# Three feed-forward stages start their first gate block on x before the norm's division, with VectorE forming every low part

## What is computed

```
x = first_block(x)                    # ffn, mixer, ffn, final norm
for i in range(2):                    # second block
    mod = silu(c) @ mod_w[i] + mod_b[i]               # 1024 x 9216, one row
    sh1, sc1, g1, sh2, sc2, g2, sh3, sc3, g3 = split(mod, 9)
    h = rmsnorm(x, g) * (1 + sc) + sh
    x = x + 0.5 * g1 * ((silu(h @ Wg) * (h @ Wu)) @ Wd)   # 1024 -> 2816 -> 1024
    ...                               # mixer, second ffn of the layer
return rmsnorm(x, final_gain)
```

## Time and profile before

| | us |
|---|---|
| median of 3 runs | 1616.53 |
| the runs | 1615.57, 1616.53, 1620.67 |
| span of the profiled execution | 1619.2 |
| its own time | not listed apart; of the three runs only 1620.67 is above its span, 1.5 over it |
| PE busy in it | 1605.0 |
| DVE busy | 1221.3 |
| ACT busy | 807.2 |

### The profile page before, as it was taken

How to read it: one execution, slowest core, us unless ns; L and a number is a source line. 1 busy time by engine, 2 the same in 40 slices (tenths; PEclk the granted TensorE clock), 3 DMA queues, 4 the chain that set the end, 5 groups by cost and what they waited for, 6 DMA issues and landing times.

```text
span 1619.2 us, 33790 instructions
## 1 busy us (share of the span) xinstructions
PE 1605.0 (99%) x14157; PEld 1583.5 (98%) x14157; DVE 1221.3 (75%) x1382; ACT 807.2 (50%) x892; POOL 48.4 (3%) x81
## 2 busy tenths in 40 slices
PE   9999999999999999999999999999999999999998
PEld 9999999999999999999998999999999998899998
DVE  6888786676778878887777888877889578774544
ACT  5434567654644354443567654445444466654343
POOL 0000000000000000000000000000000010000000
PEclk9999999999999999999999999999999999999999
DMA  8788544444568865888453368874798535345551
GB/s 327 289 305 306 219 175 171 150 156 160 184 255 294 311 224 209 316 326 295 153 183 130 131 246 327 304 292 160 288 342 316 195 139 197 135 157 206 183 197 63
DMA packets 51066, 365.04 MB, mean 225 GB/s; under 512 B 5792, under 2 KB 5920, under 8 KB 7072
## 3 DMA queue, kind: packets, MB, share of 16 engines
q1 hardware_dynamic: 40176, 287.03, 48.5%
q0 software_dynamic: 10368, 75.50, 12.8%
q10 hardware_dynamic: 432, 1.20, 0.2%
HBM read 362.65 MB, written 1.05 MB: 225 GB/s over the span
## 4 chain that ended last, share of the span: by engine, by line
PE 95%; DVE 2%; ACT 1%; DMA 1%; issue 1%; DVEq 0%; SPq 0%; ACTq 0%
PE bank L261 54%; PE bank L297 27%; PE bank L253 3%; PE bank L280 2%; PE bank L2149 1%; PE bank L384 1%; DVE wlo L192 1%; PE bank L395 1%; DMA raw<-stream_in 0%; PE bank L1652 0%; PE bank L429 0%; PE bank L2195 0%; PE bank L2101 0%; PE bank L2119 0%; PE bank L1130 0%
## 5 line engine op out<-in xcount | busy, mean ns | idle before, releaser
L261 PE MATMUL bank<-xh,whi 128*128 128x256 f32 x2608 | 725.3, 278 | 1.3 <-DVE wlo L192 1.3
L261 PE MATMUL bank<-xl,whi 128*128 128x256 f32 x2608 | 721.6, 277 | 0.0
L261 PE MATMUL bank<-xh,wlo 128*128 128x256 f32 x2608 | 721.5, 277 | 0.0
L192 DVE TENSOR_TENSOR wlo<-raw,whi 128x2048 fp32r<-128x2048 f32 x254 | 580.9, 2288 | 180.5 <-ACT whi L184 180.2
L184 ACT ACTIVATE whi<-raw 128x2048 fp32r<-128x2048 f32 x253 | 482.8, 1913 | 277.3 <-PE bank L261 166.4
L261 PEld LDWEIGHTS bank<-xh,whi 128*128 128x128 f32 x2608 | 489.9, 188 | 2.6 <-DVE wlo L192 1.7
L261 PEld LDWEIGHTS bank<-xl,whi 128*128 128x128 f32 x2608 | 490.3, 188 | 0.1
L261 PEld LDWEIGHTS bank<-xh,wlo 128*128 128x128 f32 x2608 | 489.9, 188 | 0.0
L297 PE MATMUL bank<-hid_hi,whi 128*128 128x256 f32 x1056 | 292.1, 277 | 0.0
L297 PE MATMUL bank<-hid_lo,whi 128*128 128x256 f32 x1056 | 291.6, 276 | 0.0
L297 PE MATMUL bank<-hid_hi,wlo 128*128 128x256 f32 x1056 | 291.6, 276 | 0.0
(11 more groups left out here) (392 smaller groups left out, 1842.8 us busy)
## 6 DMA issues: line engine op xcount, KB each, us to landing
raw<-stream_in SPq DMA_DIRECT2D x269, 1024.0 KB, 4.9
mod_raw<-mod_in POOLq DMA_DIRECT2D x72, 1024.0 KB, 7.6
params<-params_in SPq DMA_DIRECT2D x1, 1474.0 KB, 9.5
x<-x_in SPq DMA_DIRECT2D x2, 512.0 KB, 4.7
raw<-stream_in SPq DMA_DIRECT2D x2, 512.0 KB, 6.6
m_gsu<-sgu_in ACTq DMA_DIRECT2D x1, 1024.0 KB, 4.7
y_out<-y_tiles SPq DMA_DIRECT2D x4, 256.0 KB, 2.9
consts<-consts_in SPq DMA_DIRECT2D x1, 280.5 KB, 7.2
```

What stands on the lines that cost most here:

```text
L192: dve.tensor_tensor(wlo[:, s, :], raw[:, s, :], whi[:, s, :].bitcast(F32), ALU.subtract)\
L261: last = pe.matmul(out[:, m, :], (whi, wlo)[wp][:, s, k * 256 + m * P:k * 256 + m * P + P], (xh, xl)[ap][:, k, :], start=(k == 0 and j == ...
```

## The change

- A list `AHEAD = (6, 7, 9)` names three stages. In these PE has no `pe_norm`. Block F0 runs on `uh` and `ul`, the high and low part of `gmod * x` (gain and modulation, without 1/rms and shift). Two more columns of `uh` hold the shift's two parts, so the matmuls on `uh` have 258 columns and give W times shift beside the rest. Results go to the banks ACC[0] and ACC[1]. After the 32 matmuls on `uh` comes one matmul with ones for the sum of squares, then the 16 on `ul`.
- 1/rms is formed as in stages 0 and 2, of a 128 x 256 tile. Block F0+1 and all later ones run on the divided x, as before; DVE forms that x behind the eight parts of `ul`.
- DVE forms `wlo` of F0+1 in one piece behind four parts of `ul`, and `wlo` of F0+2 between the parts of `xl`. It scales F0's result and adds up the shift columns (two small reductions), and ACT applies silu to the two halves with the shift as bias.
- The first turn of stages 6, 7 and 9 has no modulation. `MOD_GROUPS` goes from 3, 3, 4, 4, 4 to 4, 4, 4, 3, 3 groups, so stages 0 and 2 have mod in all turns but the first, the last one included.
- The tables of stage 7 come behind the first hidden values, on DVE and on ACT, and before the splits of F0+4.
- Semaphores are shared under common names, and POOL's loop is cut by stage.

```diff
           ("final", 1, 0)]
 TABLES_AT = 7
 FACTOR_LATER = (0, 2)
+AHEAD = (6, 7, 9)
 X_TILES = ((0, 2), (2, 4), (4, 6), (6, 8))
 X_STEPS = len(X_TILES)
-MOD_GROUPS = {0: 3, 1: 3, 2: 4, 3: 4, 4: 4, 5: 0}
-GAIN_AFTER_STORE = (7,)
+MOD_GROUPS = {0: 4, 1: 4, 2: 4, 3: 3, 4: 3, 5: 0}
+GAIN_AFTER_STORE = ()
...
+        (_, uh, ul) = region(u_gap=([P, 24, T], F32), uh=([P, KD, T + 32], F32R), ul=([P, KD, T], F32R))
+        shift_cols = rstats[:, 0, 0:2]
...
         def act_split_halves(act, n):
+            if n in AHEAD:
+                act_split(act, first_block[n] + 1)
...
-                if next_stage(n) in FACTOR_LATER:
+                if next_stage(n) in AHEAD:
+                    dve_between_residuals(dve, next_stage(n), b)
+                elif next_stage(n) in FACTOR_LATER:
...
+        def dve_between_residuals(dve, n, b):
+            layer, j = MOD_OF[n]
+            if b == 1:
+                dve.wait_ge(sem("u_rounded"), (KD + 1) * u_index[n] + 1)
+                dve.tensor_tensor(uh[:, :, T + 1:T + 2], mod_col(layer, j).unsqueeze(2), uh[:, :, T:T + 1].bitcast(F32),
+                                  ALU.subtract).then_inc(sem("u_split"), 1)
+            if b >= 1:
+                dve_pair(dve, n, b - 1)
+        def dve_tree(dve, n, to, of, pairs):
+            dve.wait_ge(sem("x_paired"), paired_before[n] + pairs)
+            dve.tensor_tensor(xm[:, to, :], xm[:, to, :], xm[:, of, :], ALU.add).then_inc(sem("x_paired"), 1)
+        def act_ahead(act, n):
+            layer, j = MOD_OF[n]
+            shift = mod_col(layer, j)
+            F0 = first_block[n]
+            act.activation(std[:, 8:9], cols[:, 64:65], ACT.Sqrt)
+            act.wait_ge(sem("gmod_ready"), 2 + sum(m < n for m in MOD_OF))
+            act.activation(uh[:, :, T:T + 1], shift.unsqueeze(2), ACT.Copy).then_inc(sem("u_rounded"), 1)
+            for b, (k0, k1) in enumerate(X_TILES):
+                act.wait_ge(sem("x_updated"), X_STEPS * (last_stage(n) + 1) - X_STEPS + b + 1)
+                act.activation(xm[:, k0:k1, :], x[:, k0:k1, :], ACT.Square, scale=D ** -0.5).then_inc(sem("x_squared"), 1)
+                for k in range(k0, k1):
+                    act.activation(uh[:, k, 0:T], x[:, k, :], ACT.Identity, scale=gmod[:, k:k + 1]).then_inc(sem("u_rounded"), 1)
+            act_root(act, n)
+            act_split(act, F0 + 2)
+            for k in range(KD):
+                act.wait_ge(sem("xn_ready"), ready_before[n] + k + 1)
+                act.activation(xh[:, k, :], xm[:, k, :], ACT.Identity, bias=shift[:, k:k + 1]).then_inc(sem("xn_rounded"), 1)
+            act_split(act, F0 + 3)
+        def pe_ahead_block(pe, n):
+            s = slot_of(first_block[n])
+            pe.wait_ge(sem("w_lo_ready"), first_block[n] + 1)
+            pe.wait_ge(sem("x_updated"), X_STEPS * (last_stage(n) + 1) - X_STEPS + 2)
+            pe.wait_ge(sem("u_split"), (KD + 1) * u_index[n] + 1)
+            for part in range(2):
+                for k in range(KD):
+                    pe.wait_ge(sem(("u_rounded", "u_split")[part]), (KD + 1) * u_index[n] + k + 2)
+                    for m in range(2):
+                        c = k * 256 + m * P
+                        if part == 0:
+                            for w in (whi, wlo):
+                                pe.matmul(ACC[m][:, 0:T + 2], w[:, s, c:c + P], uh[:, k, 0:T + 2],
+                                          start=(k == 0 and w is whi), stop=False, skip_group_check=True)
+                        else:
+                            last = pe.matmul(ACC[m][:, 0:T], whi[:, s, c:c + P], ul[:, k, :], start=False,
+                                             stop=(k == KD - 1), skip_group_check=True)
+                if part == 0:
+                    pe.wait_ge(sem("x_paired"), paired_before[n] + N_PAIRS + 3)
+                    pe.matmul(STAT[:, 0:T], ones, xm[:, 0, :], start=True, stop=True, skip_group_check=True)\
+                      .then_inc(sem("x_summed"), 1)
+            last.then_inc(sem("w_used"), 1)
+        def dve_ahead(dve, n):
+            layer, j = MOD_OF[n]
+            shift = mod_col(layer, j)
+            def remainders(k0, k1):
+                for k in range(k0, k1):
+                    dve.wait_ge(sem("u_rounded"), (KD + 1) * u_index[n] + k + 2)
+                    dve.scalar_tensor_tensor(out=ul[:, k, :], in0=x[:, k, :], scalar=gmod[:, k:k + 1],
+                                             in1=uh[:, k, 0:T].bitcast(F32), op0=ALU.mult, op1=ALU.subtract)\
+                       .then_inc(sem("u_split"), 1)
+            dve_tree(dve, n, 0, 2, 3)
+            remainders(0, 2)
+            dve_pair(dve, n, 3)
+            dve_tree(dve, n, 4, 6, 5)
+            dve_tree(dve, n, 0, 4, 6)
+            remainders(2, 4)
+            dve_split(dve, first_block[n] + 1)
+            remainders(4, 5)
+            dve.wait_ge(sem("std_ready"), norm_index[n] + 1)
+            dve.reciprocal(rstd[:, :], std[:, :]).then_inc(sem("rstd_ready"), 1)
+            remainders(5, 8)
+            dve.wait_ge(sem("rstd_ready"), norm_index[n] + 1)
+            for k in range(KD):
+                dve.scalar_tensor_tensor(out=xm[:, k, :], in0=x[:, k, :], scalar=gmod[:, k:k + 1], in1=rstd[:, :],
+                                         op0=ALU.mult, op1=ALU.mult).then_inc(sem("xn_ready"), 1)
+            for k in range(KD):
+                dve.wait_ge(sem("xn_rounded"), 8 * split_index[n] + k + 1)
+                dve.scalar_tensor_tensor(out=xl[:, k, :], in0=xm[:, k, :], scalar=shift[:, k:k + 1],
+                                         in1=xh[:, k, :].bitcast(F32), op0=ALU.add, op1=ALU.subtract)\
+                   .then_inc(sem("xn_split"), 1)
+                if k == 3:
+                    dve_split(dve, first_block[n] + 2)
+            dve_split(dve, first_block[n] + 3)
+            dve.tensor_scalar(gres[:, :], mod_col(layer, j + 2), 1.0 if j == 3 else 0.5, None, ALU.mult)\
+               .then_inc(sem("gres_ready"), 1)
+            dve_gain(dve, next_stage(n))
+            dve.wait_ge(sem("w_used"), first_block[n] + 1)
+            if f_of[n]:
+                dve.wait_ge(sem("hid_ready"), STEPS * f_of[n])
+            for m in range(2):
+                dve.tensor_reduce(shift_cols[:, m:m + 1], ACC[m][:, T:T + 2], AX.X, ALU.add).then_inc(sem("bank_scaled"), 1)
+                dve.tensor_tensor(gate[:, m, :], ACC[m][:, 0:T], rstd[:, :], ALU.mult).then_inc(sem("bank_scaled"), 1)
...
         def pe_ffn(pe, n, f, groups):
             F0, S0 = first_block[n], STEPS * f
-            pe_norm(pe, n)
+            if n not in AHEAD:
+                pe_norm(pe, n)
...
+            if n in AHEAD:
+                pe_ahead_block(pe, n)
+                pe_in(pe, F0 + 1, pair(UP), first_pass_waits=8 * split_index[n])
+            else:
+                pe_in(pe, F0, pair(GATE), first_pass_waits=8 * split_index[n])
+                pe_in(pe, F0 + 1, pair(UP))
...
-                pe.wait_ge(sem("silu_done"), S0 + 1 + q + 2 * i)
+                if not (n in AHEAD and apart):
+                    pe.wait_ge(sem("silu_done"), S0 + 1 + q + 2 * i)
                 pe_in(pe, b, pair(GATE), i, 6)
...
         def act_ffn(act, n, f, groups):
             F0, S0 = first_block[n], STEPS * f
+            if n in AHEAD:
+                act_ahead(act, n)
+            else:
...
-            silu(F0)
-            act_split(act, F0 + 3)
-            if n == TABLES_AT:
-                act_tables(act)
-            round_hidden(S0, 0)
+            if n in AHEAD:
+                act.wait_ge(sem("bank_scaled"), 2 * STEPS * len(FACTOR_LATER) + 4 * u_index[n] + 4)
+                for m in range(2):
+                    ins = act.activation(gate[:, m, :], gate[:, m, :], ACT.Silu, bias=shift_cols[:, m:m + 1])
+                ins.then_inc(sem("silu_done"), 1)
+                round_hidden(S0, 0)
+                if n == TABLES_AT:
+                    act_tables(act)
+            else:
...
-            dve_phase_norm(dve, n)
...
-            dve_split(dve, F0 + 2)
-            if n == TABLES_AT:
-                dve_tables(dve)
-            dve_split(dve, F0 + 3)
+            if n in AHEAD:
+                dve_ahead(dve, n)
+            else:
+                dve_phase_norm(dve, n)
+                dve_split(dve, F0 + 2)
+                dve_split(dve, F0 + 3)
...
             post(F0 + 1, S0, 0)
-
-            def turn(i, with_mod, last):
+            if n == TABLES_AT:
+                dve_tables(dve)
+            def turn(i, with_mod, last, ahead=0):
                     g0 = group0[f]
                     for q in range(2):
-                        b = F0 + 2 + 3 * q
+                        b = F0 + 2 + 3 * q + 6 * ahead
...
             more = F0 + 33 < N_BLOCKS
+            first = n in AHEAD
+            if first:
+                turn(0, False, False)
             if groups:
                 with dve.Fori(0, groups) as i:
-                    turn(i, True, False)
-            if groups < 5:
```

(23 more changed lines are left out.)

58 lines of the change are left out of this document (30 added, 28 removed).

## The result

| | before | after |
|---|---|---|
| median of 4 runs, us | 1618.6 (1615.57 to 1621.08) | 1652.31 (1649.88 to 1657.66) |
| ratio of the times | | 1.0216, 95% interval 1.0191 to 1.0241 |
| span of the profiled execution, us | 1619.2 | 1656.0 |
| its own time, us | 1620.67 | 1657.66 |

What follows compares the result with a forecast made beforehand. PE, busy 1605.0 of 1619.2 us, bounds the kernel, so only its pauses and new waits count. 2.3 + 2.3 + 7.9 + 6.8 + 6.2 + 3 = 28.5 us more gives a median of 1645.0, range 1633 to 1655.

Steps and rivals of the forecast that it cites:

- The border (+2.3 a stage): Start of stages 6 and 9: DVE's 17.8 us queue makes F0+4 start 2.3 us later in each.
- `xl` 4 comes at +17.7, the last at +18.9: Border, F0+1: times after the last out block when DVE delivers these parts, freeing PE for F0+2 at +19.1.
- the far end of 0.38: Block on `uh`: the 258-column matmuls might take 0.38 us each, adding up to 8.5 us to PE's work.
- The tables (+7.9): Stage 7: tables on DVE delay F0+4's rounding and split to +35.7, costing 7.9 us, 5.8 of it new wait.
- The last mod turn (+6.2 at the fold): Stages 0 and 2: DVE's lag of 1.84 us a turn makes PE wait at the fold, 6.2 us later.
- The 0.6 by which the last residual was to be late: End of stage 0: DVE's last residual comes some 0.6 us behind PE, making that stage cost 6.8 us.
- I take 2 us for stage 7 and 0.5 us each for stages 0 and 2: Clock term: PE at half clock behind the new waits costs 3 us in all, between 0 and 3 each.
- the 1639 to 1650 that had 0.63: Whole kernel: the forecast's main range for the time in us, given a chance of 0.63.
- the wider range: Whole kernel: 1633 to 1655 us, taking in the case of the clock falling at every pause.
- rival 1: Borders, tables, stages 0 and 2: clock falls at every pause, 5 to 9 us more, about 1652; chance 0.17.
- Rivals 2, 3 and 4: Mod turns hidden, 1631, chance 0.10; borders not held by DVE, 1601, 0.05; gains cancel losses, within 5 us, 0.05.
- The pitch of VectorE: Border: rows give 3.22 us for 8 instructions; the skill's drain rule, 3.8, would make it some 2 us longer.

Runs made afterwards that it cites:

- e2_border9: The changed border in stage 9 alone, with group counts, tables and stages 6 and 7 as in the kernel before: 1621.66 us, ratio 1.0015.
- e10_two_reciprocals: e2_border9 with the reciprocal of stage 9 computed twice on VectorE: 1622.5 us, ratio 1.0032.
- e9_no_low_f2: e2_border9 with VectorE forming only 16 of 2048 columns of the low part of F0+2 in stage 9: 1619.37 us, ratio 1.0009.
- e3_apart7: The changed kernel with one more small identity matmul behind the first out block of stage 7: 1650.68 us, ratio 1.0199.
- e1_mod_only: The kernel before with only the change's mod group counts (4, 4, 4, 3, 3): 1635.82 us, ratio 1.0116.
- e11_mod_warm: e1_mod_only with small identity matmuls filling PE's waits for hid_lo and the fold in stages 0 and 2: 1631.16 us, ratio 1.0087.

## Why the prediction was right or wrong

- **The border (+2.3 a stage): right.** Measured +2.5 (stage 9), +3.0 (stage 6), and +2.5 alone in e2_border9. On the prediction's own clock, from the end of the last out block, e2_border9 has the reciprocal end at +9.2 (forecast +9.1), the last `xl` at +18.8 (+18.9) and F0+4 start at +30.4 (+30.1). That what lies ahead of `xm` counts in full is shown by e10_two_reciprocals. The step "`xl` 4 comes at +17.7, the last at +18.9" made the split of F0+2 count in full as well; F0+1 ended with the last `xl` in all three stages, but what leaving the split out gives, e9_no_low_f2 could not settle. PE's waits for `ul` were 3.2 us a stage rather than 5, and for `xl` 0.8 in stage 6 and nothing in stages 7 and 9 rather than 2. PE came to them later: the matmuls of 258 columns start every 0.12 us (0.113 was taken, and the far end of 0.38 did not come), the sum of squares takes 0.7, and the last six matmuls on `ul` and a part of F0+1 run at half clock. The lateness came in part as slow matmuls in place of idle time.
- **The tables (+7.9): right.** F0+4 of stage 7 came 7.9 us late, and its wait was 5.55 (forecast 5.8). The tables ended at 1164.58, 31.1 us behind the last out block, and the split at +35.7, both as forecast.
- **The last mod turn (+6.2 at the fold): right.** 195.8 was forecast, 195.81 measured, and the same 6.2 in stage 2. Of that the wait for `hid_lo` was 1.7 instead of 3.0 and the one at the fold 2.9: `hid_lo` ended at 189.85 as computed, but PE came to it 1.4 us later than the step supposed, after a wait of 0.4 for `wlo` and blocks at the slow pace. The 0.6 by which the last residual was to be late lies within the 1.7 us behind the fold.
- **"I take 2 us for stage 7 and 0.5 us each for stages 0 and 2": the term that failed, by its size.** The half clock cost 1.9 us in F0+4 of stage 7 as taken, but 1.7 stand behind the fold in each of stages 0 and 2 (with the 0.6 of the residual in the first); 1.5 of them are the 24 matmuls behind the fold, at half clock. The term held nothing for the pace at full clock, which cost 5.7 us, and nothing for the three borders (some 0.7 in stage 6, of which 0.2 are the slow pace of F0+2). Together about 11 us where 3 stood. That is all but 0.2 of the 8.3 us by which the profiled executions differ from the sum.
- **On the median** it reads +33.7 against 28.5. Of the 7.3 us between 1645.0 and 1652.31, 2.1 are the median of before, which stood at 1618.6 over four runs and not 1616.53. 1652.31 lies outside the 1639 to 1650 that had 0.63, and inside the wider range only because that took in rival 1. How much of the 5.7 us of slow pace is in the typical execution is not known; e3_apart7, which removes it, is 1.6 lower by medians.
- **Rival 1** named the right cause for the miss, the clock behind every wait, and nearly the right time (1652). But its price was of half clock alone, in all places; the largest single piece was the slow pace after it. The slices of the page, used against it, cannot show a clock that is low for 3 to 7 of 41 us: the mean of such a slice is still above nine tenths.
- **Rivals 2, 3 and 4** fell with e1_mod_only (+13.0 in the span from the mod turns alone) and e2_border9.
- **The pitch of VectorE.** The rows decided it rightly (3.25 us for eight in e2_border9 too). But the place that the prediction names (the Trainium skill, "VectorE: DVE Perf Modes", section "The DRAIN you can't avoid") says in the same paragraph that a next op that is not held starts earlier. So the 0.40 us do not speak against it, and the border longer by 2 us does not follow from it.

## What to carry to other kernels

A pause of PE at a border is worth removing only if the engine that must then deliver has the time: add up its queue up to the first operand of the second block, with every instruction in full, before moving work ahead. A wait of PE can cost more than its length again, in the matmuls behind it: in the profiled execution of the changed kernel 5.55 us of wait were followed by 7.6 us of slower matmuls. Filling the waits with small matmuls (e11_mod_warm), or placing one matmul of another kind behind one (e3_apart7), gave part of that back in the traces; in the medians the intervals overlap.

## What the runs showed of the hardware that was not expected

- **Two paces at one clock.** At a granted clock of 1.00 and without any wait, the same 48 matmuls of 256 columns take 5.44 or 5.65 us, for more than 150 us on end. In stage 7 of the changed kernel the blocks were at 5.65 behind a wait, until a matmul of another kind came (the fold; in e3_apart7 one on the identity, 0.07 us); taking that matmul away at a border where the pace was already slow left a whole stage at 5.65. A long wait or half clock is not needed, and a matmul of another kind is not the only end. In stage 0 of the changed kernel, at clock 1.00, the matmuls start every 0.118 us from 165.54 on, where PE had waited 0.44 us for `wlo`, and again every 0.113 behind the next wait, of 0.16 us at 177.07, with no other matmul between. A wait of 0.43 us at the same place of stage 2 (at 585.72) brought no slow pace. What in PE keeps the pace, and which waits bring it, was not found.
- **The time at half clock behind equal waits varies.** The wait of 3 us in F0 was followed by full clock 1.6 us into F0+1 in e2_border9 and 4.6 us in e9_no_low_f2, which differs by the length of one instruction of VectorE; F0+4 of stage 7 took 7.38 us behind a wait of 5.55 in the changed kernel and 8.49 in e3_apart7 behind one of 5.4; behind the fold e1_mod_only paid 2.8 us more than before in one stage and nothing more in the other.
- **GpSimd holds off VectorE's instructions with two inputs in SBUF**: a 4.6 us subtraction on GpSimd stretched a VectorE instruction, 0.18 us long in e2_border9, to 3.05 us, and left the reciprocal, with one input, at its 1.75.
